# Levels 1 to 4 of blocked triangular inversions in 32 by 32 blocks on TensorE

## What is computed

```python
    L = jnp.where(strict, jnp.einsum('bhnid,bhnjd->bhnij', k_beta, k) * decay, 0.0)
    eye = jnp.eye(C, dtype=F32)
    tinv = lax.linalg.triangular_solve(eye + L, jnp.broadcast_to(eye, L.shape), left_side=True, lower=True)
    u_c = tinv @ v_beta
    w_c = tinv @ (k_beta * jnp.exp(gc)[..., None])
```

## Time and profile before

| | |
|---|---|
| median of the runs | 2178.46 us |
| the profiled execution | 2178.67 us |
| its span | 2176.7 us |
| PE / PEld busy | 94% / 86% |
| DVE / ACT / POOL busy | 52% / 42% / 33% |
| RWKV loop | 184 to 318 us of the span |
| delta blocks | about 698 to 745 and 745 to 790 us |

### The profile page before, as it was taken

One profiled execution on the slowest core, in us unless ns is written; L12 is line 12 of the kernel. 1 busy time (PEld: TensorE's weight loads), 2 busy tenths in 40 slices (PEclk: granted clock), 3 DMA queues, 4 the chain that ended last, 5 costly groups with the idle time before them and its releaser, 6 DMA issues.

```text
span 2176.7 us, 40478 instructions
## 1 busy us (share of the span) xinstructions
PE 2051.6 (94%) x17526; PEld 1868.1 (86%) x17526; DVE 1138.9 (52%) x2177; ACT 911.2 (42%) x1331; POOL 709.2 (33%) x316
## 2 busy tenths in 40 slices
PE   3998999999999998999999999999999999999998
PEld 3786777889998887899999896799989998868897
DVE  6236645764483447654542447654264417357652
ACT  0452222544555425544333554333343336444443
POOL 0270000413683004136314560321561166313134
PEclk9998999999999999999999999999999999999999
DMA  8475334355443014554444440354445443314552
GB/s 323 190 294 222 128 134 150 142 188 194 155 173 138 3 40 155 190 181 154 176 174 175 153 157 22 126 174 175 170 146 175 175 174 136 136 48 151 190 194 78
DMA packets 49681, 340.48 MB, mean 156 GB/s; under 512 B 6368, under 2 KB 8416, under 8 KB 8672
## 3 DMA queue, kind: packets, MB, share of 16 engines
q1 hardware_dynamic: 49504, 337.90, 42.6%
HBM read 336.83 MB, written 1.05 MB: 155 GB/s over the span
## 4 chain that ended last, share of the span: by engine, by line
PE 84%; DVE 7%; ACT 3%; DMA 2%; issue 2%; POOL 1%; SPq 0%; ACTq 0%; POOLq 0%; DVEq 0%
PE bank L548 84%; DMA ada_ring<-ada 2%; POOL ring_low L2716 1%; PE bank L554 1%; DVE arena L2024 1%; DVE arena L2418 1%; DVE arena L2011 1%; DVE ZZ L2265 0%; DVE arena_parts L2047 0%; ACT high L1533 0%; DVE XX L2274 0%; DVE arena L2253 0%; POOL acc L2760 0%; ACT arena_parts L1558 0%; DVE acc L2117 0%
## 5 line engine op out<-in xcount | busy, mean ns | idle before, releaser
L548 PE MATMUL bank<-arena_parts,high 128*128 128x272 f32 (+2 forms) x4512 | 1019.2, 313 | 34.0 <-ACT arena_parts L1558 27.8
L548 PEld LDWEIGHTS bank<-arena_parts,high 128*128 128x128 f32 x4512 | 744.2, 190 | 83.6 <-issue 36.2
L548 PE MATMUL bank<-arena_parts,ring_low 128*128 128x272 f32 (+2 forms) x2736 | 778.6, 287 | 0.0
L1533 ACT ACTIVATE high<-ring 128x2048 fp32r<-128x2048 f32 x237 | 453.2, 1914 | 604.9 <-PE bank L548 589.4
L2716 POOL TENSOR_TENSOR ring_low<-ring,high 128x2048 fp32r<-128x2048 f32 x105 | 484.2, 4616 | 559.8 <-ACT high L1533 520.1
L548 PEld LDWEIGHTS bank<-arena_parts,ring_low 128*128 128x128 f32 (+1 forms) x2736 | 519.0, 190 | 1.2
L2060 DVE TENSOR_TENSOR ring_low<-ring,high 128x2048 fp32r<-128x2048 f32 x132 | 304.5, 2307 | 180.2 <-ACT high L1533 180.2
L548 PE MATMUL bank<-hidden_high,high 128*128 128x256 f32 (+1 forms) x1056 | 303.1, 287 | 0.0
L548 PE MATMUL bank<-hidden_low,high 128*128 128x256 f32 (+1 forms) x1056 | 301.0, 285 | 0.0
L548 PE MATMUL bank<-hidden_high,ring_low 128*128 128x256 f32 (+1 forms) x1056 | 300.2, 284 | 0.0
L2716 POOL TENSOR_TENSOR hidden_low<-arena,hidden_high 128x256 fp32r<-128x256 f32 (+1 forms) x132 | 111.7, 849 | 575.4 <-DVE hidden_high L2076 575.2
(11 more groups left out here) (332 smaller groups left out, 2160.5 us busy)
## 6 DMA issues: line engine op xcount, KB each, us to landing
ring<-stream SPq DMA_DIRECT2D x269, 1024.0 KB, 4.8
ada_ring<-ada SPq DMA_DIRECT2D x48, 1024.0 KB, 6.1
con<-consts SPq DMA_DIRECT2D x1, 1542.5 KB, 11.4
con<-consts SPq DMA_DIRECT2D x1, 1040.0 KB, 6.9
arena<-xin SPq DMA_DIRECT2D x1, 1024.0 KB, 11.5
out<-arena SPq DMA_DIRECT2D x2, 512.0 KB, 2.9
prob_even<-consts SPq DMA_DIRECT2D x1, 384.0 KB, 11.9
par<-params SPq DMA_DIRECT2D x1, 272.5 KB, 9.3
```

What stands on the lines that cost most here:

```text
L548: ins = nc.tensor.matmul(o, l, r, start=start, stop=stop_, skip_group_check=True)
L1533: act(high[:, q % HIGHS], ring[:, s % RING], ACT.Copy).then_inc(a.sig(high_ready), 1)
```

## The change

Levels 1 to 4 no longer work on the whole 64x64 matrices. They stay inside the four diagonal blocks of 32 by 32 that stand under each other on 128 partitions (`quarter_rows`); a unit takes 32 columns instead of 64. `XD32` holds both forms of the blocks' inverses, `XF` the finished 64x64 inverse, in the space that `XR` had. A product of 64x64x64 becomes two of 32x32x32; four consecutive ones use four diagonal 32x32 tiles of TensorE. What was level 5 becomes `middle_of_halves` and `merged_halves`, which work out the off-diagonal quarter of 32x32 and put the inverse together.

```diff
@@ turn_unit, PE
-                    for cc in range(2):
-                        rows = half_rows(cc)
-                        last = u == 3 and cc
-                        m = mm(bank[g][rows, 64 * u:64 * u + 64], XR[rows, g, u // 2, u % 2, 1], ident[rows, rows], True,
-                               True, hold=last)
+                    for r in range(4):
+                        rows, last = quarter_rows(r), u == 3 and r == 3
+                        m = mm(bank[g][rows, 32 * u:32 * u + 32], XD32[rows, g, u, 1], ident[rows, rows], True, True, hold=last)
@@ middle, PE
+                    for r in range(4):
+                        rows, last = quarter_rows(r), u == 3 and r == 3
+                        o = 32 * (r % 2)
+                        m = mm(bank[g][rows, 32 * u:32 * u + 32], GRAM[rows, g, u // 2, u % 2, 0, o:o + 32],
+                               XD32[rows, g, u, 0], True, True, hold=last)
+            def middle_of_halves(g):
+
+                eng.wait_ge(inverse_step[g], pe.nth(inverse_step[g]))
+                for u in range(4):
                     for cc in range(2):
-                        rows = half_rows(cc)
-                        last = u == 3 and cc
-                        m = mm(bank[g][rows, 64 * u:64 * u + 64], GRAM[rows, g, u // 2, u % 2, 0, 0:64],
-                               XR[rows, g, u // 2, u % 2, 0], True, True, hold=last)
+                        upper, lower, last = quarter_rows(2 * cc), quarter_rows(2 * cc + 1), u == 3 and cc
+                        m = mm(bank[g][lower, 32 * u:32 * u + 32], GRAM[upper, g, u // 2, u % 2, 0, 32:64],
+                               XD32[upper, g, u, 0], True, True, hold=last)
@@ merged, PE
-                    if l < 5:
-                        for cc in range(2):
-                            rows = half_rows(cc)
-                            mm(bank[b][rows, P * u:P * u + 64], XR[rows, g, u // 2, u % 2, 1], ZR[rows, g, u], True, True)
+                    for r in range(4):
+                        rows = quarter_rows(r)
+                        mm(bank[b][rows, 64 * u:64 * u + 32], XD32[rows, g, u, 1], ZR[rows, g, u], True, True)
+                    for r in range(4):
+                        rows, last = quarter_rows(r), u == 3 and r == 3
+                        m = mm(bank[b][rows, 64 * u + 32:64 * u + 64], ZR[rows, g, u], XD32[rows, g, u, 1], True, True, hold=last)
+            def merged_halves(g):
+
+                b = 2 + g
+                eng.wait_ge(middle_ready[g], pe.nth(middle_ready[g]))
+                for u in range(4):
                     for cc in range(2):
-                        rows = half_rows(cc)
-                        last = u == 3 and cc
-                        m = mm(bank[b][rows, P * u + 64:P * u + P], ZR[rows, g, u], XR[rows, g, u // 2, u % 2, 1], True,
-                               True, hold=last)
+                        upper, lower, last = quarter_rows(2 * cc), quarter_rows(2 * cc + 1), u == 3 and cc
+                        mm(bank[b][upper, 32 * u:32 * u + 32], ZR[lower, g, u], XD32[lower, g, u, 1], True, True)
+                        m = mm(bank[b][lower, 32 * u:32 * u + 32], ident[lower, lower], XD32[lower, g, u, 1], True, True, hold=last)
@@ the RWKV loop, PE
-                for l in range(1, 6):
+                for l in range(1, 5):
                     for g in range(2):
                         middle(g, l)
                     for g in range(2):
                         merged(g, l)
-                    if l < 5:
-                        stream_slab(slab + l - 1)
+                    stream_slab(slab + l - 1)
+                for g in range(2):
+                    middle_of_halves(g)
+                for g in range(2):
+                    merged_halves(g)
@@ the turned form, ACT, in both mixers
-                    act(XR[:, g, :, :, 0], bank[g][:, 0:256].rearrange("p (e c f) -> p e c f", e=2, c=2), ACT.Copy).then_inc(a.sig(turned_ready[g]), 1)
+                    act(XD32[:, g, :, 0], bank[g][:, 0:128].rearrange("p (u f) -> p u f", u=4), ACT.Copy).then_inc(a.sig(turned_ready[g]), 1)
@@ masked, DVE
-                    nv.tensor_tensor(XR[:, g, e, :, 1], gram[:, 0:4:2, 0:64], over_tiles(mask64("first64"), 2, 64),
+                    mine = slice(2 * e, 2 * e + 2)
+                    nv.tensor_tensor(XD32[:, g, mine, 1], gram[:, 0:4:2, 0:32], over_tiles(mask64("first64", 32), 2, 32),
+                                     ALU.mult).then_inc(v.sig(vstep), 1)
+                    nv.tensor_tensor(XF[:, g, mine, 0:32], gram[:, 0:4:2, 32:64], over_tiles(mask64("first64")[:, 32:64], 2, 32),
                                      ALU.mult).then_inc(v.sig(free["vector"][b]), 1)
                 eng.wait_ge(*v.last)
-                x = XR[:, g, :, :, 1]
-                nv.tensor_tensor(x, x, bank[g][:, 256:512].rearrange("p (e c f) -> p e c f", e=2, c=2),
+                x = XD32[:, g, :, 1]
+                nv.tensor_tensor(x, x, XF[:, g, :, 0:32], ALU.add).then_inc(v.sig(vstep), 1)
+                eng.wait_ge(*v.last)
+                nv.tensor_tensor(x, x, bank[g][:, 256:384].rearrange("p (u f) -> p u f", u=4),
                                  ALU.add).then_inc(v.sig(unit_ready[g]), 1)
@@ middle and merged, DVE
-                nv.tensor_tensor(ZR[:, g], bank[g][:, 0:256].rearrange("p (u f) -> p u f", u=4),
-                                 four_units(mask64(f"merge64_{l}"), 64), ALU.mult).then_inc(v.sig(middle_ready[g]), 1)
+                nv.tensor_tensor(ZR[:, g], bank[g][:, 0:128].rearrange("p (u f) -> p u f", u=4),
+                                 four_units(mask64(f"merge32_{l}", 32), 32), ALU.mult).then_inc(v.sig(middle_ready[g]), 1)
-                first = 0 if l < 5 else 1
-                x = XR[:, g].rearrange("p e c x f -> p (e c) x f")[:, :, first:2]
-                y = bank[2 + g][:, :].rearrange("p (u x f) -> p u x f", u=4, x=2)[:, :, first:2]
+                x = XD32[:, g]
+                y = bank[2 + g][:, 0:256].rearrange("p (u x f) -> p u x f", u=4, x=2)
                 nv.tensor_tensor(x, x, y, ALU.add).then_inc(v.sig(inverse_step[g]), 1)
+            def middle_of_halves(g):
+
+                eng.wait_ge(full_for_vector[g], v.nth(full_for_vector[g]))
+                nv.tensor_copy(ZR[:, g], bank[g][:, 0:128].rearrange("p (u f) -> p u f", u=4)).then_inc(v.sig(middle_ready[g]), 1)
+            def merged_halves(g):
+
+                nv.tensor_scalar(XF[:, g, :, 0:32], XD32[:, g, :, 1], cm("own_half", 1, 0), None, ALU.mult).then_inc(v.sig(vstep), 1)
+                eng.wait_ge(full_for_vector[2 + g], v.nth(full_for_vector[2 + g]))
+                nv.tensor_copy(XF[:, g, :, 32:64], bank[2 + g][:, 0:128].rearrange("p (u f) -> p u f", u=4)).then_inc(v.sig(inverse_step[g]), 1)
```

More of the change, by code:

```diff
@@ L477, in half_rows, with quarter_rows @@
             return slice(64 * h, 64 * h + 64)
+        def quarter_rows(r):
+            return slice(32 * r, 32 * r + 32)
         def xview(T):
@@ L979, in solve @@
                             last = e and cc
-                            m = mm(bank[b][rows, P * e:P * e + P], XR[rows, g, e, tau, 1], SIDES[g][rows, tau, e], True,
+                            m = mm(bank[b][rows, P * e:P * e + P], XF[rows, g, 2 * e + tau], SIDES[g][rows, tau, e], True,
                                    True, hold=last)
@@ L1237, in _ @@
                             rows, last = half_rows(cc), u == 3 and cc
-                            m = mm(bank[b][rows, P * u:P * u + P], XR[rows, g, u // 2, u % 2, 1],
+                            m = mm(bank[b][rows, P * u:P * u + P], XF[rows, g, u],
                                    DTOK[rows, 0, 2 * g + u // 2, u % 2], True, True, hold=last)
@@ L1246, in _ @@
                             m = mm(bank[6 + cc][:, 256 * g + 64 * u:256 * g + 64 * u + 64], DTOK[rows, 1, 2 * g + u // 2, u % 2],
-                                   XR[rows, g, u // 2, u % 2, 1], True, True, hold=last)
+                                   XF[rows, g, u], True, True, hold=last)
                             if last:
@@ L2306, in _ @@
                         grown_learned_keys(1)
-                    if i == 1 and l == 5:
-                        grown_keys(1)
+                for g in range(2):
+                    middle_of_halves(g)
+                for g in range(2):
+                    merged_halves(g)
+                if i == 1:
+                    grown_keys(1)
                 modulation(FIRST + PROJECTION_PIECES + 1 + i, 7)
@@ L2489, in _ @@
                     eng.wait_ge(*v.last)
-                    x = XR[:, g, :, :, 1].rearrange("p e c f -> p (e c) f")
-                    nv.tensor_tensor(x, mine[:, :, 0:64], four_units(mask64("first64"), 64), ALU.mult).then_inc(v.sig(vstep), 1)
+                    x, rest = XD32[:, g, :, 1], XF[:, g, :, 0:32]
+                    nv.tensor_tensor(x, mine[:, :, 0:32], four_units(mask64("first64", 32), 32), ALU.mult).then_inc(v.sig(vstep), 1)
```

(9 more changed lines are left out.)

19 lines of the change are left out of this document (13 added, 6 removed).

## The result

The changed kernel takes 2243.74 us in the median (2243.22 to 2247.18), against 2178.46: slower by 3.0%, a ratio of 1.0303 with a 95% interval from 1.0276 to 1.0329. Its profiled execution also took 2243.74, with a span of 2241.7 us. Forecast were 2222.1 us and a range from 2192 to 2254. Direction and mechanism came as forecast; 21.6 us of the loss were not in my sum, and most of this part is about them.

What follows compares the result with a forecast made beforehand. TensorE was taken to bound the kernel, and after the change the arrival of its 256-instruction pages: 2178.7 + 30.6 (RWKV loop) + 12.8 (delta blocks) = 2222.1 us, range 2192 to 2254.

Steps and rivals of the forecast that it cites:

- The bound: TensorE sets the pace, busy 94%; it stalls where a 256-instruction page ends, a page taking 3.5 to 3.9 us to come.
- The count of instructions: Six places with inversions: 224 more products, 896 more PE instructions (3.5 pages) in each; some 21 more packets.
- TensorE's own time: Inversion levels, instructions always there: 32x32 tiles start 8 ns apart; middle 0.26 us for 0.47, merged 0.51 for 0.97.
- DVE: Inversion levels: masked copy 423 to 280 ns, addition 687 to 423; masks gain 0.6 us for two groups.
- A page in the delta blocks: Two delta blocks: 6.4 pages at 3.8 us make 24.3 us for 17.9, +12.8 us for both.
- what follows the blocks gives nothing back: Stage behind each delta block: it waits for the block's results, so it hides none of the added time.
- A page in the RWKV loop: Four RWKV iterations: 9.1 pages at 3.85 us plus 6.2 make 41.2 us for 33.6, +30.6 us in all.
- Pages arrive ahead: Rival on instruction fetch: several pages are in store, so the sum without page limit holds, 2148 us; chance 0.09.
- Small tiles don't overlap: Rival on 32x32 products: pairs take 30 ns, +68 us with the turning, 2247 us; chance 0.05.
- A colder clock: Rival: idling PE falls to 1.2 GHz, some 5 us more an RWKV iteration, 2245 us; chance 0.08.

Runs made afterwards that it cites:

- e_burst: Kernel before plus 512 one-column products (32x32 weights, 2048 TensorE instructions) in one row ahead of the first delta block's first turning: 2210.52 us.
- e_count64: Kernel before plus 224 one-column products (64x64 weights, shape and order of the real ones) at each of six places: 2259.43 us.
- e_again: The changed kernel run once more with nothing altered: 2247.83 us (2239.32 to 2260.47), 1.0312 of before.
- e_middle: Kernel before with only the middle products of levels 1 to 4 on diagonal 32x32 tiles, all else as before: 2181.74 us, 1.0009 of before.
- e_half: Changed kernel with middle and merged products of levels 1 to 4 over two units at a time, 48 products a level for 96: 2178.39 us.
- e_count: Kernel before plus 224 one-column products (32x32 weights) at each of six places, spread between the real products of old tiles: 2438.71 us.

## Why the prediction was right, and where its sum fell short

**The bound.** Right. The reading of two issue pieces at multiples of 256 as the end of a page carried the whole forecast, and e_burst repeats it seven times in a row.

**The count of instructions.** Right: 5376 more, 21 packets.

**TensorE's own time.** Forecast: 8 ns a pair of 32x32. Where the clock was full, it is that; where it was 0.50, 13. In the changed kernel, a merged stretch that changes clock while it runs:

```profile
288.02 0.31 PE L555 MATMUL bank<-XX,ZZ 32*32 32x32 f32 x8
288.13 0.31 PE L555 MATMUL bank<-ZZ,XX 32*32 32x32 f32 x8
...
288.64 0.20 PE L555 MATMUL bank<-ZZ,XX 32*32 32x32 f32 x4
...
288.70 0.20 PE L555 MATMUL bank<-XX,ZZ 32*32 32x32 f32 x4
```

8 in 0.11 us, 13 to 14 ns each, while one takes 0.31; then 8 from 288.64 to 288.70 (4, and 1 and 3 that are left out here), 8 ns each, while one takes 0.20. The working behind the 8 was looser than its result: I took a pair's 60 ns per tile of 64 as 53 for the columns and 7 for the rest, and e_count64 says that a pair of one column costs 26 ns on two tiles, so the columns are not what sets the 30. The 8 came out all the same, and that is luck. The 25 ns floor that the Trainium skill gives ("TensorE: Matmul & The Clock Gate", Part 1) is near what two tiles show there, and is passed by four.

**DVE.** Right within the reading: 291 ns for the masked copy (forecast 280), 421 for the addition (423). The masks of an iteration stand in the chain from 275.62 to 280.47, 4.85 us, against 4.19 before (218.74 to 222.93), +0.66 for a forecast of 0.6.

**A page in the delta blocks.** Right: 24.9 and 25.2 us against 24.3. **The step after them failed:** "what follows the blocks gives nothing back" was said of hidden time, and I did not ask what it may take. The blocks are 7.0 and 7.3 us longer, 14.3 for 12.8. Behind each the solve ran at the lower clock, 1.7 us more for its first 32 matmuls and 0.6 for the next ones, and some executions lose 11 to 13 us in the chain of chunks in addition. So the stage cost 17 us in this profile and 28 in e_again's, against 12.8. That the stalls cause the 11 us is not shown: e_middle loses 5.6 in that place without them.

**A page in the RWKV loop.** 41.2 us an iteration were forecast, 45.0 came. The term that was mis-sized is the page time of 3.85: it was read from three packets in a window in which no other transfer shows. 45.0 us an iteration are (45.0 - 6.2) / 9.1 = 4.3 us a page, the part that the cold clock may have in it included. I had its price in the bounds (4.4 us a page, +50 us, for "packets that wait behind a slab's copy") and chose against it, at 3.85. With the copies gone the iteration takes 40.2 us and the loop costs 32.3 for my 30.6; with them 48.5. So the upper end was the likelier value, for a reason that I had written down: each level asks for a copy, and a level is as long as a page and a half.

**The rivals.** "Pages arrive ahead" needed issue pieces to be something else; they were not. The Trainium skill says of the crossing of a 16 KB boundary that it is mostly hidden ("Runtime: NRT & Kernel Launch", Instruction fetch mechanics). The trace agrees only as long as 256 instructions last over 3.65 us, and the depth found in e_burst is one page ahead. "Small tiles don't overlap" is refuted by the 8 ns and by e_half. "A colder clock" was treated as another case, with 0.08, at 2245 us; it was none of another case but a companion of the forecast one: PE that waits for pages is PE that idles. I had even its condition, "PE would idle over half of a level". A consequence of the likeliest case belongs in its sum.

**The range.** 2192 to 2254 held the time. It did so through its upper part, which the 4.4 us page had set. One of the four executions of e_again, the same kernel, took 2260.47 us and lies outside; the sum had nothing for a stretch that runs at either clock.

## What to carry to other kernels

Count instructions per microsecond wherever TensorE runs short products: at 256 in less than 3.65 us it starved here, and below that a cut in the work's length bought nothing, while each further instruction cost 14 ns (3.65 us / 256). Smaller diagonal tiles halve the columns and multiply the instructions, so they pay only where pages have room, and that room must be measured with the transfers of the stage in flight. When a stall is forecast, charge the stage behind it for a cold start too. And where a stage far from the change runs at either clock from one execution to the next, compare the changed stage by itself, marker to marker, before reading a total.

## What was not expected of the hardware

- Copies of 1 MB slabs in flight stretch the instruction packets from 3.3 to 4.3 us apart to as much as 6, 5 us in an iteration of ten pages, though the DMA engines are busy only 28% of that time.
- Matmuls on tiles of 32x32 and of 64x64 in turn hardly overlap: four small and four real ones take 0.41 us at the full clock where the real four alone take 0.12, and e_count, at a clock of 0.62, loses 43 us in each place.
- On two diagonal tiles of 64x64 a matmul of one column costs 26 ns, nearly as much as one of 64 (30 ns).
- The granted clock fell to 0.62 in e_count with PE shown busy 99%, and to 0.50 in e_burst.
- The lower clock can last while PE is busy: in e_again 28 us at 0.50 with PE busy 27.48 us of them, in another execution of the same kernel 1.00 in that place. It is 11 us in one stage, more than the 10.2 us by which the two profiled executions differ. e_middle shows the same stretch in part at 0.50 without a page stall ahead of it. That it also makes the other executions of the changed kernel range from 2239 to 2260 us is likely, but they have no trace.
